# The opening of a two-layer decoder step: input loaded first, fp32 conditioning in four column groups, and the first products by fours of k tiles

## What is computed

```python
def adaln(c, w, b):
    mod = jax.nn.silu(c) @ w + b
    shift, scale, gate = jnp.split(mod[:, None, :], 3, axis=-1)
...
        hp = rmsnorm(xp, g_pre[l]) * (1.0 + sc_p) + sh_p
        hs = rmsnorm(xs, g_pre[l]) * (1.0 + sc_s) + sh_s
...
def attention_branch(h, w_in, w_out, sinks, buf_k=None, buf_v=None):
    proj = h @ w_in
```

## Time and profile before

| | us |
|---|---|
| median of 3 runs | 2597.72 (2597.67 to 2603.41) |
| the profiled execution: span | 2596.8 |
| its own time, by the span and the 0.9 us by which the median of the runs exceeds it | about 2597.7 |
| PE busy | 2449.3 (94% of the span) |
| DVE busy | 1213.0 (47%) |
| ACT busy | 875.6 (34%) |
| the mean granted TensorE clock | 0.951 |
| read from and written to HBM | 274.81 MB, 27.56 MB |

### The profile page before, as it was taken

How to read it: one execution, slowest core, us unless ns; L and a number is a source line. 1 busy time by engine, 2 the same in 40 slices (tenths; PEclk the granted TensorE clock), 3 DMA queues, 4 the chain that set the end, 5 groups by cost and what they waited for, 6 DMA issues and landing times.

```text
span 2596.8 us, 42451 instructions
## 1 busy us (share of the span) xinstructions
PE 2449.3 (94%) x17089; PEld 2259.8 (87%) x17089; DVE 1213.0 (47%) x1739; ACT 875.6 (34%) x1303; POOL 65.2 (3%) x108
## 2 busy tenths in 40 slices
PE   5979999999999899999699999999999999989996
PEld 4679989889898598888499999999999999988996
DVE  6663453543544645553943343333343434355424
ACT  5732342332432445553431222121212222234322
POOL 1000000000000000000000000000000000000000
PEclk9989999999999599999899989899999999989998
DMA  8863222222121047777254966774649556616731
GB/s 324 306 211 94 76 55 64 71 66 85 50 68 49 1 151 234 238 242 223 76 111 68 83 85 96 68 98 74 98 66 88 95 88 76 96 50 211 247 81 69
DMA packets 346795, 300.84 MB, mean 116 GB/s; under 512 B 9585, under 2 KB 288361, under 8 KB 345497
## 3 DMA queue, kind: packets, MB, share of 16 engines
q1 hardware_dynamic: 336976, 247.88, 44.9%
q0 software_dynamic: 9360, 50.19, 5.3%
q10 hardware_dynamic: 290, 0.27, 0.0%
HBM read 274.81 MB, written 27.56 MB: 116 GB/s over the span
## 4 chain that ended last, share of the span: by engine, by line
PE 82%; DMA 7%; DVE 5%; ACT 3%; issue 2%; DVEq 1%; ACTq 0%; SPq 0%
PE PJ L746 57%; DMA arena<-in_w_ada 3%; PE MX L938 3%; PE MX L864 3%; PE MX L885 3%; DMA raw<-in_w_in_mlstm 3%; PE PJ L711 2%; PE MX L871 2%; PE MX L1060 1%; PE MX L1070 1%; DMA raw<-in_w_in_attn 1%; PE MX L828 1%; PE MX L1022 1%; DVE strips L1788 1%; DMA obuf<-in_w_ada 1%
## 5 line engine op out<-in xcount | busy, mean ns | idle before, releaser
L746 PE MATMUL PJ<-h_hi,w_hi 128*128 128x272 f32 x4384 | 944.3, 297 | 39.0 <-DVE h_lo L1579 24.7
L746 PE MATMUL PJ<-h_hi,w_lo 128*128 128x272 f32 x4384 | 922.1, 292 | 0.0
L746 PE MATMUL PJ<-h_lo,w_hi 128*128 128x272 f32 x4384 | 920.9, 292 | 0.1
L746 PEld LDWEIGHTS PJ<-h_hi,w_hi 128*128 128x128 f32 x4384 | 713.8, 193 | 73.6 <-issue 38.6
L746 PEld LDWEIGHTS PJ<-h_lo,w_hi 128*128 128x128 f32 x4384 | 705.8, 193 | 0.0
L746 PEld LDWEIGHTS PJ<-h_hi,w_lo 128*128 128x128 f32 x4384 | 701.3, 193 | 0.2 <-issue 0.2
L1521 DVE TENSOR_TENSOR w_lo<-raw,w_hi 128x2048 fp32r<-128x2048 f32 x106 | 242.9, 2292 | 406.5 <-ACT w_hi L1159 406.4
L1159 ACT ACTIVATE w_hi<-raw 128x2048 fp32r<-128x2048 f32 x106 | 202.0, 1905 | 42.1 <-DMA raw<-in_w_in_mlstm 34.6
L1788 DVE TENSOR_TENSOR strips<-arena,strips 128x1024 fp32r<-128x1024 f32 x128 | 153.1, 1223 | 82.2 <-ACT strips L1349 80.4
L1349 ACT ACTIVATE strips<-arena 128x1024 fp32r<-128x1024 f32 x128 | 131.4, 1060 | 107.9 <-DMA arena<-in_w_ada 107.5
L938 PE MATMUL MX<-strips,cT 128*128 128x512 f32 x512 | 141.9, 399 | 17.9 <-DVE strips L1788 17.9
(11 more groups left out here) (303 smaller groups left out, 2137.1 us busy)
## 6 DMA issues: line engine op xcount, KB each, us to landing
arena<-in_w_ada SPq DMA_DIRECT2D x128, 512.0 KB, 5.0
raw<-in_w_in_mlstm SPq DMA_DIRECT2D x64, 1024.0 KB, 14.8
raw<-in_w_in_attn SPq DMA_DIRECT2D x40, 1024.0 KB, 5.6
obuf<-in_w_ada SPq DMA_DIRECT2D x32, 1024.0 KB, 7.8
raw<-in_w_out_attn SPq DMA_DIRECT2D x16, 1024.0 KB, 7.8
raw<-in_w_out_mlstm SPq DMA_DIRECT2D x16, 1024.0 KB, 6.5
x_spill<-arena POOLq DMA_DIRECT2D x2, 4352.0 KB, 12.3
arena<-x_spill POOLq DMA_DIRECT2D x2, 4352.0 KB, 17.7
```

Source lines behind the costliest of these rows:

```text
L746: last = mm(PJ[:, 2 * pair + f, 0:HT], w, h[:, k, HT * f:HT * f + HT], start=(k == 0 and n == 0), stop=(k == KT - 1 and n == 2))
```

## The change

- SP loads all five tiles of x before anything else: four to a buffer of their own, `x_rows` (in the place of `h_lo`), the fifth to `raw[0]`.
- The conditioning of layer 0 works on the raw fp32 weights, without rounding or splitting. `c4` holds for each k tile the 9 columns of c, filled up to 32 with zeros. A unit is now a whole DMA of 4 k tiles: four fp32 matmuls, the one of k tile i into the PSUM partitions 32i to 32i + 31 (`ada_unit`). ACT copies all 128 partitions (`mod_copy`), and `ada_turn` adds the four groups up by a selection matrix `sel` of 128 x 9. The bias comes from a turned table `bT`, which DVE adds (`mod_empty`). SP's next DMA waits for the unit four before it (`a0_used`).
- The eight groups come in the order 0, 4, 1, 5, 2, 6, 3, 7, so that each pair completes shift and scale of four k tiles.
- Transposes of x and the sums of squares write to PJ, the conditioning to MX.
- All of x is turned during group 0, and the squares are summed during group 1.
- The weights of entries 0 and 1 are loaded between units 7 and 8, and rounded and split before the first part.
- Norm and modulation go in four parts of four k tiles (`first_part`, `first_modulate`), over small buffers `tmp` and `smp`; after each, PE makes these four k tiles of entries 0 and 1 (`first_entries`), in groups 2, 4 and 6 of the conditioning after their third unit, and at the end.
- The spill of x waits for the 28th unit.

The core of the diff:

```diff
+FIRST_ADA = [0, 4, 1, 5, 2, 6, 3, 7]
...
-            sp.wait_ge(c_in, 32)
+            for t in range(5):
+                src = x_prompt[0, P * t:P * t + P, :] if t < 4 else x_sample.rearrange("b t d -> (b t) d")
+                sp.dma_start(x_tile(t), src).then_inc(x_in[t], 16)
             for u in range(32):
                 if u >= 4:
-                    sp.wait_ge(lo_done, 2 * (u - 3))
-                if u == 28:
-
-                    sp.wait_ge(xt_done, 5)
+                    sp.wait_ge(a0_used, u - 3)
+                if u == 8:
+
                     for e in range(2):
                         load_entry((None, 0), e)
...
+            pool.wait_ge(a0_used, 28)
             pool.wait_ge(xe_a, 10)
             pool.wait_ge(xe_d, 10)
             pool.dma_start(x_spill, xflat).then_inc(spilled, 16)
...
+            def ada_unit(e, q):
+
+                u = 4 * e + q
+                pe.wait_ge(a0_in[q], 16 * (e + 1))
+                if q == 0 and e >= 2:
+                    pe.wait_ge(mod_copied, e - 1)
+                for i in range(4):
+                    last = mm(MX[32 * i:32 * i + 32, e % 2, :], c4[:, 4 * q + i, :], a0_slot(u)[:, i, :],
+                              start=(q == 0), stop=(q == 3))
+                last.then_inc(a0_used, 1)
...
+            def first_entries(g):
+
+                for e in range(2):
+                    if g == 0:
+                        pe.wait_ge(ms_ready, 1)
+                        pe.wait_ge(lo_done, e + 1)
+                    pe.wait_ge(hs_ready, g + 1)
+                    block(slot_of("l0", e), pair_of("l0", e), {}, 0, range(4 * g, 4 * g + 4))
+
+            turn_x(0)
+            turn_x(1)
+            for q in range(4):
+                ada_unit(0, q)
+                if q < 3:
+                    turn_x(q + 2)
+            for q in range(4):
+                ada_unit(1, q)
+                if q == 1:
+                    ada_turn(0)
+                sums(0, range(4 * q, 4 * q + 4))
+            for e in range(2, 8):
+                for q in range(4):
+                    ada_unit(e, q)
+                    if q == 0:
+                        ada_turn(e - 1)
+                    if q == 2 and e % 2 == 0:
+                        first_entries(e // 2 - 1)
+            ada_turn(7)
+            first_entries(3)
...
+            mod_empty(0)
+            mean_square(1)
             dve.wait_ge(sink_in, 16 * 9)
             chain(ts(nsink[:, :], nsink[:, :], -1.0, None, ALU.mult))
-            gain(0)
-            norm_split(0, 1)
+            inverse(1)
+            mod_empty(1)
+            for e in range(2):
+                split_lo("l0", it0, e)
+            for g in range(4):
+                first_part(g)
+                if g < 3:
+                    mod_empty(2 * g + 2)
+                    mod_empty(2 * g + 3)
```

More of the change, by code:

```diff
@@ L194, in trunk @@
         h_hi = sb("h_hi", [P, KT, T], F32R)
+        with nc.sbuf_tensor("x_rows", [P, 4, D], F32) as x_rows:
+            pass
         h_lo = sb("h_lo", [P, KT, T], F32R)
@@ L292, in trunk @@
         sink_in = sem("sink_in")
-        x_in = [sem("x_in0"), sem("x_in1")]
+        x_in = [sem(f"x_in{i}") for i in range(5)]
+        a0_used = sem("a0_used")
         a0_in = [sem(f"a0_in{i}") for i in range(4)]
@@ L450, in load @@
                 s = slot_of(ph, e, j)
-                if not (ph == "l0" and it[0] is None and e < 2):
+                if ph == "l0" and it[0] is None and e < 2:
+                    sp.wait_ge(xt_done, 5)
+                else:
                     split = fixed(sp, unit_no(ph, it, e, j - 1))
@@ L559, in _, with bias @@
             brow = misc[50:51, 0:512]
-            def bias(a, first=False):
-                if not first:
-                    pool.wait_ge(mod_turned, a)
+            def bias(a):
+                pool.wait_ge(mod_turned, a)
                 pool.dma_start(brow, bada[:, ds(a * 512, 512)]).then_inc(bias_in, 16)
[L566 to L587, removed]
+            pool.dma_start(nsink[:, 0:QH], sinks.broadcast_to([P, QH])).then_inc(sink_in, 16)
+            for a in range(2):
+                for bl in range(2):
+                    src = sinks.rearrange("o (m a l h) -> (o a l) m h", m=GR, a=2, l=2)[2 * a + bl]
+                    p0 = 64 * a + 32 * bl
+                    for h in range(2):
+                        dst = nsink[p0:p0 + 32, QH + 4 * h:QH + 4 * h + 4]
+                        pool.dma_start(dst, src[:, h:h + 1].rearrange("m h -> h m").broadcast_to([32, GR]), **SLOW)\
+                            .then_inc(sink_in, 16)
+            pool.wait_ge(a0_used, 28)
             pool.wait_ge(xe_a, 10)
@@ L734, in entry, with block @@
                 block(s, pair, points, h_base)
-            def block(s, pair, points, h_base):
-                if h_base in (0, 2 * KT):
-                    pe.wait_ge(hs_ready, h_base // (2 * KT) + 1)
-                for k in range(KT):
+            def block(s, pair, points, h_base, ks=range(KT)):
+                if h_base == 2 * KT:
+                    pe.wait_ge(hs_ready, 5)
+                for k in ks:
                     if h_base is not None:
@@ L913, in layer0 @@
             def layer0(it, prev, h_base=None):
-                for e in range(len(L0K)):
+                for e in range(2 if h_base == 0 else 0, len(L0K)):
                     points = {}
@@ L1363, in _ @@
             root(3)
[L1364 removed]
+            modulate()
             round_hi("l1", it0, 0)
```

284 lines of the change are left out of this document (141 added, 143 removed).

## The result

The changed kernel took **2583.56 us** (median of 20 runs), the kernel before 2600.95 us beside it (20 runs): ratio **0.994**, 95% interval 0.9927 to 0.9953, or 17.4 us less. A second comparison on another chip gave 2586.82 against 2594.57, ratio 0.9973 (0.9956 to 0.999). The forecast was 28 us less. So the direction was right, and the gain came out at 17.4 us in the first comparison and 7.8 in the second.

What follows compares the result with a forecast made beforehand. The body was taken as a rigid block of matrix work, so only time before entry 4 counts. Entry 4 moves from 204.3 to 176.3, saving 28.0 us: 2597.7 - 28.0 = 2569.7, said as 2570 us, range 2555 to 2584.

Steps and rivals of the forecast that it cites:

- step 2: Conditioning unit of four fp32 matmuls: column groups overlap, 0.95 us, 1.8 at the lower clock.
- Step 1: Opening, x loaded first: x landed by 14.2 us, PE starts on it at 14.5, x in place at 30.
- step 6: Spill of x starts with unit 31's load; queues alternate by packet, unit 31 lands at 135.4 us, against 125.3 alone.
- Steps 3 and 4: Sums of squares end at 51 us; root, copy, reciprocal and splits at 61.1, first modulation part at 68.4.
- Step 5: PE waits for the first part, holding buffers: unit 15 lands at 79.3 us instead of 63.7, unit 27 used at 120.
- the first rival: Lower clock throughout: every hold's tiles and the x stage at 1.2 GHz, 7 us in all, 2577 us; chance 0.17.
- Step 7: End of the opening: entry 2 starts at 152.1 us, entry 3 at 164.2 (weights land at 144), entry 4 at 176.3.
- the mark: Start of entry 4 of layer 0: 204.3 us in the kernel before, forecast at 176.3, 28.0 us earlier.
- Serial groups: Rival: column groups run one behind the other, unit 3.44 us, PE becomes the bound, 2610 us, slower; chance 0.06.
- pairs: Rival: only two column groups overlap at a time, between 2590 and 2605 us; chance 0.05.
- The free stream: Rival: nothing holds the weight loads, last unit lands at 104.6, 30.8 us earlier, 2539 us; half of it 2555; chance 0.10.
- The lower clock: The first rival: holds and x stage at 1.2 GHz, each hold about 2 us longer, 2577 us; chance 0.17.

Runs made afterwards that it cites:

- Run 3: Changed kernel with all four matmuls of a unit in one column group: 2628.18 us.
- Run 7: POOL's eight single-sink loads replaced by VectorE copies: on the changed kernel 2576.42 us, ratio 0.9929; on the combination 2559.83 us, ratio 0.9869.
- the combination: Changed kernel with the eight small loads on SP's queue ahead of x and the spill after unit 11: 2570.81 us, ratio 0.9909; repeated 2573.82 us, 0.9924.
- run 4: Changed kernel with parts 0 to 2 of the first entries four units later: 2588.24 us, ratio 0.9979.
- run 6: On the combination: x before unit 0, 2570.82 us; parts four units later with ACT's copy first and spill after unit 12, 2571.23; both, 2572.94.
- Run 2: Changed kernel with the spill of x waiting for 11 units instead of 28: 2578.15 us, ratio 0.9926.
- experiment 1: Changed kernel with SP holding back x and conditioning weights until ACT's eight small loads have landed: 2577.53 us, ratio 0.9929.
- run 5: Changed kernel with the eight small loads on SP's queue ahead of x: 2579.81 us, ratio 0.9952; with spill after unit 11 too, 2570.81 us, 0.9909.

## Why the prediction was right and wrong

*The unit, step 2: right.* 0.95 and 1.8 us were forecast, 1.07 and 1.94 measured from first start to end. Run 3 shows that this is the four groups side by side, 3.44 us in one group. The drain at each change of the tiling mode that the Trainium skill has (TensorEngine Tiling (Array Packing), Key Properties) shows next to no price here. In the chain the unit begins at 55.10, where the sums' 3.96 from 51.14 end, and takes 1.00 us between two changes of the mode, against 1.85 for two units in a row (49.28): under 0.1 us for both changes. By the 2.38 that the Trainium skill gives for three groups (TensorE: Matmul & The Clock Gate, Why this matters for your kernels) the unit would have been 1.45 us, an estimate; the trace has 1.00, so four groups are worth 3.44 / 1.00 = 3.4.

*Step 1, "c's chain ends as before at 13.8 so PE starts on x at 14.5", and "with a start near 3 us it is in by 14.2": wrong, 16.5 us and 13 us.* This is the largest miss. I took the order of issue for the order of landing and priced x at 408 GB/s, the rate of a stretch without other queues. The change put x's large packets beside POOL's tiny ones, at the pace of these. Before, the same stretch held the conditioning weights to 45 GB/s, and I had not asked what TensorE's 12.4 us of idle time ahead of 25.25 waited for. The packet counts that I used in step 6 were the very rule that I left out in step 1. Run 7 shows the cause: without POOL's eight loads x is in at 19.2, and with the small loads ahead of it on SP's queue its last tile is turned at 30.4, where step 1 had 30.

*x's first two tiles* took 3.7 us each (30.98 and 36.20 in the chain), the later ones 1.95; forecast 1.9 for all. That the first two ran at 1.2 GHz is read from this pace alone: the windows say 1.00 there, but the trace's clock records begin at 40.0. It is 3.5 us more; in run 7 on the combination only the first tile was slow (3.42).

*Steps 3 and 4: right in their lengths.* From unit 4 (50.2) to the end of the sums (70.9) it took 20.7 us, forecast 21. Splits end at 80.6 and part 0's last matmul at 92.05: all 19 us late, with the opening.

*Step 5, the hold: right.* A lone unit took 5.2 us from issue to landing (unit 15 93.10 to 98.34, unit 23 118.34 to 123.56), forecast 5.3. Unit 15 was 19.0 us behind its forecast, unit 27's use 23.6: so from the first landing to the last use it took 4.6 us more than forecast. Of this, 3.5 are the lower clock, the first rival's term: behind each of the two later holds the unit and the turn take 1.94 + 1.82 us, where 0.95 + 1.05 stood. Another 2.4 are the second unit behind each hold, which lands 3.8 us after the first and not 2.6, and 1.3 came back in the parts. What the first hold costs no run shows: runs 4 and 6 meant to take it away, but in both the spill met units in flight (20.53 and 18.55 us for one load).

*Step 6, "they alternate by packet, unit 31 lands at 135.4, against 125.3 alone": wrong, 8.6 us the other way.* Unit 31 was issued at 143.64 and landed at 150.4, 6.7 us later; the spill, issued 0.3 us behind, took 17.9 us. Timeline of POOL of the changed kernel:

```profile
143.91 0.57 POOL L591 DMA_DIRECT2D x_spill<-arena  x1 [137.33 <-PE MX L708]
162.13 0.55 POOL L594 DMA_DIRECT2D arena<-in_const  x1 [17.66 <-DMA x_spill<-arena]
```

Its queues from 144 to 149 us and from 149 to 155 us (q0 is the spill, q1 the loads):

```profile
q1 hardware_dynamic: 462, 0.94, 76.3%
q0 software_dynamic: 2, 0.07, 3.2%
...
q0 software_dynamic: 76, 2.65, 102.4%
q1 hardware_dynamic: 128, 0.14, 6.5%
```

The spill's first packets came 4.9 us after its issue (in the kernel before 1.1 us), and by then a unit issued with it is nearly through. In run 4, where the stream had a backlog when the spill was issued, units 30 and 31 were caught behind it. The alternation that step 6 counts on was not what failed, the start of the spill was wrong.

*Step 7, "its weights are behind unit 31 in the queue and land at 144": wrong.* Here step 6's rule was not applied to the next loads in the queue. These have 512 B packets beside 34 KB ones, until 161.9, then POOL's tables and caches beside them, and landed at 165.2 and 180.5 after 21 and 36 us. Unit 31 was 15.0 us behind its forecast, entry 3 20.7. Unit 31 is no longer on the path at all: this goes from unit 27's use at 143.6 to the load for entry 3. Run 2 gives 7.7 us back.

*The sum.* 16.5 us of late start, 2.5 more up to unit 15, 4.6 up to unit 27, -8.6 at unit 31 and 5.7 behind it are 20.7 us, the whole gap between 28.0 and 7.3. These are differences of the lateness from one point of the forecast to the next, so they have to add up; runs tested the first (1, 5 and 7) and what the spill does to the last (2), not the 2.5 and the 4.6. With the losses taken out the gain at the mark is 29.4. Of these, 6.4 belong to the tiny loads that the kernel before had too, so the change itself, mended, is worth about 23 where 28 was forecast. The lower clock behind the holds stays in it (the first unit behind part 0 takes 1.93 us there as well); where all of the missing 5 are, no run shows.

*The time* of 2583.56 us lies at the very end of the range, 2555 to 2584. That is luck: this end was set by a lower clock in every hold, and what came was a late x and a late load for entry 3.

*The rivals.* Serial groups and pairs are refuted by run 3. The free stream did not come. The lower clock came in part: 3.5 us behind the two later holds. None held what decided.

## What to carry to other kernels

Price a load by what shares the DMA engines at its time, not by its bytes: count packets per queue in the window, and if the counts are equal while the shares are far below 1, look for the queue with tiny packets. Loads of single values (here eight of 4 B elements) belong in one row-wise load and a few copies on an idle engine. When a large transfer is moved, follow each load issued within its time and who waits for it, down to the second and third behind it; put the transfer where the stream stands still anyway.

## What was not expected of the hardware

- A queue of 32 B and 4 B packets, 12 ns of work each on average (1.7% of 16 engines for 67 of them in 3 us), held a queue of 8 KB packets to 22 packets per us, 145 GB/s, and one of 2 KB packets to 45 GB/s; with it gone the same stream ran at 423 GB/s. A queue of 512 B and 36 B packets did not hold x up (1.25 MB in 3 us at one packet for one). In the kernel before POOL's queue brought x in 8 KB packets, with x's first two tiles landed at 7.3 and 10.6 us, so it isn't that queue as such; whether it is the size or the scattered order of these loads was not tried. Why each DMA engine gets one of their packets only each 0.7 us (each 0.9 us in experiment 1, with nothing beside them) stays open.
- The delay can be more than one packet for one: in experiment 1 x's first packet moved 4.35 us after its issue, while only POOL's tiny packets were about; in the changed kernel it moved 1.0 us after.
- One queue's small loads, ahead of x on the same queue, landed 1.2 to 1.6 us apart with POOL's tiny loads about, and 0.0 to 0.3 us apart without (4.97, 4.98, 5.16, 5.41, 5.63 us).
- The spill moved its first packet 1.1 us after its issue in the kernel before, where the queues were empty, and 2.6 to 5.0 us after in the changed kernel and its variants, where SP's loads were in flight. What delays it there was not tried.
